# Fused two-block kernel on one core: the first stage, the ends of two loops and the mixer's loop in another order

## The chip, the cores and the metric

One core of a Trainium2 chip runs the whole kernel; the other cores are idle. The metric is the device time of one launch in microseconds (us). The engines are named as in the profile: PE is TensorE, DVE is VectorE, ACT is ScalarE, POOL is GpSimd, SP is SyncE, which only issues DMAs here.

## What is computed

Two blocks over 512 tokens of 1024 channels, all in float32. Cut to the parts at issue:

```python
# first block, layer 0 (16 heads of 128), layer 1 (Fourier, 8 groups of 256 channels)
sh, sc, gt = split(silu(cvec) @ ada_w + ada_b)            # modulation, from c and from c_ctx
h = rms_norm(x) * (1 + sc) + sh                           # for 512 tokens and for 256 context tokens
q, f1, f2, v, z = h @ w_in                                # per head
o = chunk_scan(forwards) + chunk_scan(backwards)          # gated linear recurrence
x = x + gt * ((rms_norm(o) * silu(z)) @ hg_w_out)         # E = 2048 -> D = 1024
u, z = split(h @ ft_w_in);  y = fft2(u).real * silu(z)
x = x + gt * (y @ ft_w_out)                               # E = 2048 -> D = 1024
# second block: x = x + swiglu/2; x = x + token_mixer(rms_norm(x)); x = x + swiglu/2; rms_norm
# token_mixer: six projections, 4-tap conv + RG-LRU scan, GLU + 31-tap conv + layernorm, two gates
```

## The kernel before, in words

Activations lie with channels on the 128 partitions and tokens along the free axis, so a product is made of 128x128 weight tiles against up to 512 tokens. To keep float32 accuracy each factor is split in two fp32r parts, the rounded upper half (`hi`) and the remainder (`lo`), and each tile takes three matmuls: hi x hi, hi x lo, lo x hi (`three`, L436).

**The weight stream.** All big weights come as a stream of blocks of eight tiles (512 KB, `BLK` = 1024 columns), in the order in which PE wants them. There are two slots. For each block SP loads `w_raw` when the slot's `lo` was made (L392); ACT copies it to `w_hi` (`cut`, L881) once the block two earlier in the same slot has been used (`after(k)` waits for block k and cuts block k+2); DVE subtracts to make `w_lo` (L1360); PE's `take` waits for that and its last matmul of the block frees the slot (`w_used`). Every engine works through its own list in the order that is written out in the code, and a waiting instruction holds up all behind it on its engine.

**First stage (L384 to L505, L922 to L946, L1418 to L1482).** SP loads the vectors, then x (2 MB), then four parts of the modulation weights (2 MB each). POOL loads the context (1 MB), masks, identity and the first gate weights. ACT squares x and the context, one 128x512 tile at a time through one buffer, `st_sq`, and DVE adds them up. PE computes the modulation with 64 matmuls (L498), the first mean (L480) in front of the fourth part and the second mean after all. DVE copies the four result rows out of PSUM, inverts the first root (L1462), copies the last row, makes the `lo` halves of blocks 0 and 1, adds biases, and then goes through both norms: for each tile one scalar_tensor_tensor (x times scale times inverse root, L1384), ACT makes `hi` with the shift (L901), DVE makes `lo` (L1387). The second root and its inverse stand between the two norms. PE's first real product waits for these tiles.

**Heads (a Fori of 15 and one ending).** `pe_head(i, j)` projects head i (five blocks, in parts a, b, c, and the modulation of layer 1) in between the steps of the scan of head j. The last call has no head i: there `begin_output(k, part)` puts the first half (tiles of heads 0 to 7) of the first four blocks of the output projection into parts a and b. After it come the other halves of those four (tiles of heads 8 to 15, each waits with `as_cut` until the last y is split), then four more channel tiles of two blocks each (`residual`). A channel tile that is done is added to x by DVE, squared by ACT, and the squares summed by DVE.

**Fourier mixer (a Fori of 7 groups and one ending).** `pe_group(i, j)` projects group i (four blocks, `project(0..3)`) between the transforms of group j: `turn`, `over_tokens(0, 1)`, `over_channels(0, 1)`. The last call has nothing to project. Its output projection (16 blocks) starts after all y are split (L736, `dve_ft`). Then POOL loads 64 KB of meta tokens and DVE and ACT make small sums from them before the residual starts.

**Mixer's loop (a Fori of 4, L797 on PE, L1230 on ACT, L1970 on DVE).** Each iteration uses 14 blocks: six against 528 tokens (two banks), six against 512, and two (`RG_A`, `RG_X`) of which only the first four of eight tiles hold anything. ACT does the activations, DVE a 4-tap convolution, the scan and its products, and 62 taps of the long convolution (`some_taps(n)`, one instruction each, L1963), placed by hand between the splits of blocks. PE's block k waits for `w_lo` of that block.

## Time and profile before

| what | us |
|---|---|
| median of 3 runs | 2650.39 |
| lowest and highest | 2647.41, 2652.21 |
| the profiled execution, its own time | 2652.72 |
| span in the profile | 2651.0 |
| PE busy | 2517.7 (95%) |
| DVE busy | 1629.7 (61%) |
| ACT busy | 1001.7 (38%) |

The profiled execution is one run: its own time is 1.7 us above its span. A matmul's end is modelled, so "busy" of PE counts short tails behind a last matmul; the distance from one start to the next is the surer measure. The granted clock (PEclk) is 1.00 at 2.4 GHz and 0.50 at 1.2 GHz; 0.98 is its mean over the run.

### The profile page before, as it was taken

How to read it: one execution, taken by the hardware profiler on the slowest of the kernel's cores; microseconds unless marked ns; L12 is line 12 of the kernel's file. 1: busy time of each engine (PE TensorE's matmuls, PEld its weight loads, DVE VectorE, ACT ScalarE, POOL GpSimd, SP SyncE). 2: the span in 40 equal slices, each digit the busy share in tenths (PEclk: the TensorE clock that was granted, in tenths of full speed). 3: DMA queues.
4: the chain of work that ended last, by engine and by line, in shares of the span. 5: the costliest groups of instructions: out<-in, count | busy, mean ns of one | idle time of the engine just before them, and what ended most of it. 6: DMA issues, size and time to landing. Idle time of an engine off the chain costs nothing.

```text
span 2651.0 us, 40390 instructions
## 1 busy us (share of the span) xinstructions
PE 2517.7 (95%) x14488; PEld 2172.3 (82%) x14488; DVE 1629.7 (61%) x2380; ACT 1001.7 (38%) x1350; POOL 113.7 (4%) x140
## 2 busy tenths in 40 slices
PE   6999999999999988999899999989999999999996
PEld 1788888888888875888689999989888878888885
DVE  5567777777777655444446343457999985544445
ACT  3334443444335323333235322235455543322222
POOL 0011211111111100000000000000000000000000
PEclk9999999999999998999899999989999999999998
DMA  5121222122212222222122222222222222222222
GB/s 227 64 72 57 77 71 71 56 79 71 71 55 79 95 80 65 78 72 78 49 95 86 88 90 92 87 95 88 87 84 90 90 84 95 88 95 95 95 95 87
DMA packets 59818, 223.83 MB, mean 84 GB/s; under 512 B 6496, under 2 KB 6496, under 8 KB 59264
## 3 DMA queue, kind: packets, MB, share of 16 engines
q1 hardware_dynamic: 56544, 207.94, 23.7%
q0 software_dynamic: 3232, 15.34, 1.6%
q8 instruction: 26, 0.43, 0.1%
q14 instruction: 16, 0.13, 0.0%
HBM read 221.15 MB, written 2.10 MB: 84 GB/s over the span
## 4 chain that ended last, share of the span: by engine, by line
PE 84%; DVE 7%; issue 4%; ACT 4%; DMA 1%; DVEq 0%; ACTq 0%; SPq 0%; POOL 0%
PE ps L441 73%; PE ps L600 4%; PE ps L622 1%; PE ps L498 1%; DVE w_lo L1360 1%; DVE cv L1963 1%; ACT L976 1%; DMA ada_raw<-in_ada_weights_dram 1%; PE ps L641 1%; PE ps L613 1%; PE ps L632 1%; PE ps L587 1%; PE ps L634 1%; PE ps L633 1%; DVE n_tmp L1963 0%
## 5 line engine op out<-in xcount | busy, mean ns | idle before, releaser
L881 ACT ACTIVATE w_hi<-w_raw 128x1024 fp32r<-128x1024 f32 x360 | 381.3, 1059 | 997.5 <-PE ps L441 991.9
L1360 DVE TENSOR_TENSOR w_lo<-w_raw,w_hi 128x1024 fp32r<-128x1024 f32 x360 | 439.3, 1220 | 223.8 <-ACT w_hi L881 221.7
L441 PE MATMUL ps<-n_hi,w_hi 128*128 128x512 f32 (+1 forms) x992 | 323.1, 357 | 27.9 <-DVE w_lo L1360 16.3
L441 PE MATMUL ps<-n_lo,w_hi 128*128 128x512 f32 (+1 forms) x992 | 320.3, 355 | 0.0
L441 PE MATMUL ps<-n_hi,w_lo 128*128 128x512 f32 (+1 forms) x992 | 319.9, 354 | 0.0
L441 PE MATMUL ps<-h_hi,w_hi 128*128 128x512 f32 x640 | 273.6, 427 | 8.3 <-DVE h_lo L1387 4.2
L441 PE MATMUL ps<-h_hi,w_lo 128*128 128x512 f32 x640 | 255.3, 399 | 0.0
L441 PE MATMUL ps<-h_lo,w_hi 128*128 128x512 f32 x640 | 254.9, 398 | 0.0
L441 PEld LDWEIGHTS ps<-n_hi,w_hi 128*128 128x128 f32 x992 | 175.1, 190 | 61.6 <-issue 20.5
L441 PEld LDWEIGHTS ps<-n_lo,w_hi 128*128 128x128 f32 x992 | 175.9, 190 | 27.1 <-issue 0.2
L441 PEld LDWEIGHTS ps<-n_hi,w_lo 128*128 128x128 f32 x992 | 175.9, 190 | 26.7
L441 PEld LDWEIGHTS ps<-h_hi,w_hi 128*128 128x128 f32 x640 | 121.8, 190 | 37.6 <-issue 9.6
L441 PEld LDWEIGHTS ps<-h_hi,w_lo 128*128 128x128 f32 x640 | 121.5, 190 | 29.2
L441 PE MATMUL ps<-xg_hi,w_hi 128*128 128x264 f32 x704 | 144.2, 286 | 0.0
L441 PE MATMUL ps<-xg_lo,w_hi 128*128 128x264 f32 x704 | 143.2, 285 | 0.0
L441 PEld LDWEIGHTS ps<-h_lo,w_hi 128*128 128x128 f32 x640 | 122.0, 191 | 25.1 <-issue 2.9
L441 PE MATMUL ps<-xg_hi,w_lo 128*128 128x264 f32 x704 | 142.3, 283 | 0.0
L441 PE MATMUL ps<-hid_hi,w_hi 128*128 128x264 f32 (+1 forms) x528 | 141.2, 321 | 0.0
L441 PE MATMUL ps<-hid_lo,w_hi 128*128 128x264 f32 (+1 forms) x528 | 141.0, 322 | 0.0
L441 PE MATMUL ps<-hid_hi,w_lo 128*128 128x264 f32 (+1 forms) x528 | 140.6, 320 | 0.0
L600 PE MATMUL ps<-Q,K_now 128*128 128x128 f32 x896 | 127.8, 286 | 5.3 <-ACT K_now L1008 3.6
L600 PEld LDWEIGHTS ps<-Q,K_now 128*128 128x128 f32 x896 | 118.4, 191 | 16.7 <-ACT K_now L1008 10.2
(342 smaller groups left out, 5052.7 us busy)
## 6 DMA issues: line engine op xcount, KB each, us to landing
w_raw<-in_weights_dram SPq DMA_DIRECT2D x376, 512.0 KB, 3.3
ada_raw<-in_ada_weights_dram SPq DMA_DIRECT2D x4, 2048.0 KB, 25.6
gate_raw<-in_gate_weights_dram POOLq DMA_DIRECT2D x16, 512.0 KB, 3.6
x<-in_x_dram SPq DMA_DIRECT2D x1, 2048.0 KB, 9.2
x<-in_x_dram POOLq DMA_DIRECT2D x1, 2048.0 KB, 8.0
out_dram<-fin POOLq DMA_DIRECT2D x1, 2048.0 KB, 6.5
xc<-in_ctx_dram POOLq DMA_DIRECT2D x1, 1024.0 KB, 10.6
masks<-in_masks_dram POOLq DMA_DIRECT2D x1, 512.0 KB, 12.8
```

What stands on the lines that cost most here:

```text
L441: last = nc.tensor.matmul(o, w, xp, start=start and n == 0, stop=stop and n == 2)
L498: last = nc.tensor.matmul(ps[0:2, n], csil[:, k], raw_[:, :, k * P:(k + 1) * P], start=k == 0, stop=k == KD - 1)
L587: last = nc.tensor.matmul(ps[:, 4, tile(t)], ksum[:, tile(t)], q_st[:, tile(t)], start=True, stop=True)
L600: last = nc.tensor.matmul(ps[:, 5 - l % 2, tile(t)], K_now[:, l % 2, tile(t)], woven(Q, t * P, P, 2 ** l, 1), start=True, stop=True)
L613: last = nc.tensor.transpose(ps[:, 6, tile(x)], K[:, d, tile(ORDER[d][n])], ident[:])
L622: last = nc.tensor.matmul(ps[:, 4 + g_ % 2, tile(x)], KT[:, x], V[:, ORDER[d][n]], start=True, stop=True)
L632: nc.tensor.matmul(o, V[:, CT + t], ST[:, t], start=True, stop=False)
L633: nc.tensor.matmul(o, states[:, 1 + t, 0], Q[:, 0, tile(t)], start=False, stop=False)
L634: last = nc.tensor.matmul(o, states[:, 4 - t, 1], Q[:, 1, tile(t)], start=False, stop=True)
L641: nc.tensor.matmul(ps[:, 5], ones_h[:], osq[:], start=True, stop=True).then_inc(pe_scan, 1)
L881: run(w_hi[:, s], w_raw[:, s], ACT.Copy).then_inc(hi_ready[s], 1)
L1360: tt(w_lo[:, s], w_raw[:, s], w_hi[:, s].bitcast(F32), ALU.subtract).then_inc(lo_ready[s], 1)
```

## The change

1. **First stage.** SP's queue becomes: vectors, modulation part 0, x, part 1, context, parts 2 and 3. POOL waits for the context before it loads the identity, and for part 3 before the masks. The squares go through two buffers. The mean of x stands inside part 1 of the modulation and the context's mean behind it. ACT instead of DVE copies the modulation rows. DVE multiplies x and the context by their inverse roots in place before the modulation is there (`over_root`), so that after it ACT makes `hi` straight from x with scale and shift, and DVE makes a tensor_scalar and a subtraction.
2. **Ending of the heads.** 16 half blocks instead of 8 go between the steps of the last scan: first the tiles of heads 0 to 7 of four blocks, then those of heads 8 to 13 of four more. The tiles of heads 14 and 15 (two of each block) are split into a buffer of their own, `kept`, and multiplied at the end. The tile order of SP's loads is written out (`OUT_ORDER`); it names the same blocks. ACT and DVE get `early_after(k)` at eight places.
3. **Ending of the Fourier mixer.** `begin_output(k)` puts tiles of channels 0 to 1023 of four output blocks between the transforms of the last group; their other halves come right after, and only tiles 14 and 15 wait for the last y. SP loads those blocks in the order of `OUT_ORDER`. The residual's loops there are unrolled.
4. **Mixer's loop.** The two half-empty blocks are split only in their first 512 columns. On DVE, splits move ahead of taps and between the two scans; on ACT, the split and activation of the last block move ahead of the last two copies.

```diff
-            sp.dma_start(x0[:], x_in).then_inc(x_in_s, 16)
             for n, (dst, a, b_) in enumerate(ADA_LOADS):
                 sp.dma_start(dst, ada_in[a:b_].rearrange("b p n -> p b n")).then_inc(ada_loaded[n], 16)
+                if n == 0:
+                    sp.dma_start(x0[:], x_in).then_inc(x_in_s, 16)
+                elif n == 1:
+                    sp.dma_start(xc[:], ctx_in).then_inc(xc_in_s, 16)
...
             for n, (raw_, a, b_) in enumerate(ADA_LOADS):
-                if n == 3:
-                    mean(N0, T, st_sum[:, 0])
                 pe.wait_ge(ada_loaded[n], 16)
                 for k in range(KD):
+                    if n == 1 and k == KD - 2:
+                        mean(N0, T, st_sum[:, 0])
                     last = nc.tensor.matmul(ps[0:2, n], csil[:, k], raw_[:, :, k * P:(k + 1) * P],
                                             start=k == 0, stop=k == KD - 1)
                 last.then_inc(ada_part, 1)
+                if n == 1:
+                    mean(N0C, TC, st_sum[:, 1], bank=5)
...
+            def over_root(N, x, rt_):
+                dve.wait_ge(N["root"], 1)
+                own.link(v.reciprocal(rt_, rt_))
+                for k in range(KD):
+                    tt(x[:, k], x[:, k], rt_, ALU.mult).then_inc(N["tmp"], 1)
+
+            over_root(N0, x0, st_sq[:])
             cut(0)
             cut(1)
+            over_root(N0C, xc, st_tmpc[:, 2])
...
+            def first_lo(N, x, n, tmp, hi, lo):
+                for k in range(KD + 1):
+                    if k < KD:
+                        if k > 1:
+                            dve.wait_ge(N["lo"], k - 1)
+                        own.mark(ts(tmp(k), x[:, k], scale[:, n, k:k + 1], ada0[:, k, n:n + 1], ALU.mult, ALU.add))
+                    if k:
+                        own.wait(1 if k < KD else 0)
+                        dve.wait_ge(N["hi"], k)
+                        tt(lo(k - 1), tmp(k - 1), hi(k - 1).bitcast(F32), ALU.subtract).then_inc(N["lo"], 1)
...
+                def begin_output():
+                    k, n = next(parts)
+                    xs = as_cut({"lo": y_cut}, whole(y_hi, y_lo))
+                    if n == 0:
                         s = take(k)
                         pe.wait_ge(acc_free, HEADS * 6 + 2)
+                    at, half = k // EARLY * KD, (KD - (LATE if k >= EARLY else 0)) // 2
+                    last = tiles(k % 2, [ps[:, k % EARLY]], xs, range(at + half * n, at + half * (n + 1)),
+                                 k < EARLY and n == 0, False, half * n)
+                    if n:
+                        last.then_inc(w_used[k % 2], 1)
...
+            pe.wait_ge(kept_s, EARLY)
+            for n in range(LATE):
+                t = HEADS - LATE + n
+                pe.wait_ge(y_cut, t + 1)
+                for k in range(EARLY):
+                    last = three([ps[:, k]], kept_hi[:, k, n * P:(n + 1) * P], kept_lo[:, k, n * P:(n + 1) * P],
+                                 [y_hi[:, t]], [y_lo[:, t]], False, n == LATE - 1)
+                    if n == LATE - 1:
+                        last.then_inc(early_done, 1)
...
-            st.enter(0, EARLY)
             for k in range(EARLY):
-                st.wait_done(dve, k)
+                dve.wait_ge(early_done, k + 1)
                 stt(x1[:, k], ps[:, k], gates[:, k, 0:1], x1[:, k], ALU.mult, ALU.add).then_inc(RC["res"], 1)
-                after(k)
                 add_square(RC, k, *sums)
...
-                project(0); turn(); project(1); over_tokens(0); over_tokens(1)
-                project(2); over_channels(0); project(3); over_channels(1)
+                project(0); turn(); project(1); begin_output(0); over_tokens(0); begin_output(1); over_tokens(1)
+                project(2); begin_output(2); over_channels(0); project(3); begin_output(3); over_channels(1)
...
-            pe.wait_ge(dve_ft, GROUPS * 8 + 1)
-            residual(RF, KD // 2, 2, whole(y_hi, y_lo), T)
+            for k in range(EARLY):
+                s = take(k)
+                tiles(s, [ps[:, k]], last_y, range(KD, 2 * KD), False, True).then_inc(w_used[s], 1)
+            residual(RF, (KD - EARLY) // 2, 2, whole(y_hi, y_lo), T, done=EARLY)
...
-                after(4)
+                after(4, BLK // 2)
                 for a in range(2):
                     actv(1 + a)
...
                     actv(3 + a)
                     tt(ii[:, a], ii[:, a], xr[:, a], ALU.mult)
                     stt(pp[:, a], (gvs, ggs)[a][:], 1.0, pp[:, a], ALU.add, ALU.mult).then_inc(mx_dve, 1)
-                some_taps(4)
                 after(11)
+                some_taps(3)
                 for a in range(2):
                     actv(5 + a)
                     own.link(tt(ii[:, a], ii[:, a], pp[:, a], ALU.mult))
                     own.link(v.tensor_tensor_scan(pp[:, a], rr[:, a], ii[:, a], 0.0, ALU.mult, ALU.add))
                     staged(7 + a)
                     tt(yst[:, a], yst[:, a], pp[:, a, META:TM], ALU.mult).then_inc(mx_dve, 1)
-                some_taps(2)
-                after(12)
-                some_taps(6)
+                    after(12 + a)
+                    some_taps((2, 1)[a])
                 for a in range(2):
                     actv(7 + a)
                     tt(row(a_lo, i * 2 + a), yst[:, a], row(a_hi, i * 2 + a).bitcast(F32), ALU.subtract
                        ).then_inc(mx_dve, 1)
-                after(13)
-                some_taps(7)
+                some_taps(4)
                 after(14)
-                some_taps(len(taps))
+                some_taps(6)
```

The numbers of taps between the other splits of an iteration are, in order, 5, 6, 4, 6, 4, 6, 3, 8 and 4 (before: 5, 5, 4, 6, 3, 6, 2 and 2, 2 and none); the two half splits are those of `RG_A` and `RG_X`.

## Rows read from the trace of the kernel before

**Rows 1.** The page, part 1: busy us (share of span), instructions

```profile
PE 2517.7 (95%) x14488; PEld 2172.3 (82%) x14488; DVE 1629.7 (61%) x2380; ACT 1001.7 (38%) x1350; POOL 113.7 (4%) x140
```

**Rows 2.** Busy time of each engine in stretches of the span (first line: columns)

```profile
core 0: us, PE busy (x) PEld busy (x) DVE busy (x) ACT busy (x) POOL busy (x), PEclk, DMA share, GB/s
...
20.00:36.00 16.00, 16.00 (x33) 2.93 (x32) 4.76 (x11) 3.96 (x9) 0.00 (x0) 1.00 1.02 409
...
102.20:902.90 800.70, 789.72 (x4833) 692.96 (x4832) 581.12 (x927) 342.63 (x508) 103.72 (x120) 1.00 0.21 68
902.90:981.90 79.00, 68.13 (x320) 55.75 (x319) 47.88 (x61) 23.19 (x33) 6.42 (x10) 0.91 0.31 104
...
1049.00:1270.40 221.40, 221.40 (x1142) 186.82 (x1142) 106.29 (x213) 79.29 (x134) 0.00 (x0) 1.00 0.22 74
1270.40:1293.80 23.40, 10.68 (x58) 9.72 (x56) 11.42 (x25) 6.11 (x13) 0.00 (x0) 0.71 0.07 23
...
1889.40:1970.50 81.10, 75.64 (x481) 68.02 (x481) 74.58 (x103) 43.63 (x52) 0.00 (x0) 1.00 0.28 91
...
2110.40:2168.00 57.60, 49.18 (x197) 37.63 (x196) 53.37 (x73) 22.11 (x29) 0.00 (x0) 0.97 0.25 83
```

**Rows 3.** Chain that ended last, first 103 us: start us, us, what

```profile
1.80 17.77 DMA ada_raw<-in_ada_weights_dram
...
43.77 6.97 PE ps L498 x16
...
54.13 0.76 DVE st_tmp L1384
...
77.91 24.26 PE ps L441 x120
```

**Rows 4.** Timeline of the first stage: start us, us, instruction, idle before

```profile
10.56 0.63 ACT L908 ACTIVATE st_sq<-x 128x512 f32<-128x512 f32 x1 [4.77 <-DMA x<-in_x_dram]
...
12.34 0.69 DVE L1371 TENSOR_TENSOR st_sum<-st_sum,st_sq 128x512 f32<-128x512 f32 x1 [0.69 <-ACT st_sq L908]
...
45.87 3.35 DVE L1462 RECIPROCAL st_sq<-st_sq 128x512 f32<-128x512 f32 x1 [2.44 <-ACT st_sq L895]
```

**Rows 5.** The same chain in the last head: start us, us, what

```profile
905.96 5.46 PE ps L441 x12
...
912.07 2.79 PE ps L441 x12
...
954.57 1.14 PE ps L641 x2
...
962.76 37.29 PE ps L441 x152
```

**Rows 6.** Timeline of the Fourier ending, and DVE's last sum on meta tokens

```profile
1274.77 1.94 PE L703 MATMUL ps<-ident,u_st 128*128 128x128 f32 x8 [4.22 <-DVE y_lo L1789]
...
1300.22 0.17 DVE L1858 TENSOR_SCALAR both_sum<-both_sum 128x16 f32<-128x16 f32 x1
```

**Rows 7.** The chain there: start us, us, what

```profile
1287.32 0.39 ACT o_sb L1141
...
1293.84 6.32 PE ps L441 x19
```

**Rows 8.** Waits within one iteration of the mixer's loop: us, times, longest

```profile
PE ps L441 <- DVE w_lo L1360: 5.8, 4, 2.2
...
DVE ii L2025 <- ACT gvs L1289: 2.8, 1, 2.8
```

**Rows 9.** Instructions by tile: count, ns min/median/max, first and last start, forms

```profile
L1959 DVE TENSOR_SCALAR cv<-vpad,vec x8: 545/546/548, 1807.2 to 2089.2; 128x512 f32 x8
...
L2040 DVE TENSOR_TENSOR a_lo<-yst,a_hi x8: 678/682/686, 1873.3 to 2117.0; 128x512 f32 x8
```

**Rows 10.** The page, part 5: groups, busy us and mean ns, idle before

```profile
L881 ACT ACTIVATE w_hi<-w_raw 128x1024 fp32r<-128x1024 f32 x360 | 381.3, 1059 | 997.5 <-PE ps L441 991.9
L1360 DVE TENSOR_TENSOR w_lo<-w_raw,w_hi 128x1024 fp32r<-128x1024 f32 x360 | 439.3, 1220 | 223.8 <-ACT w_hi L881 221.7
```

More of the change, by code:

```diff
@@ L53 @@
 Z_BANK = 2
+BLOCKS_TO_OUT = HEADS * 6 + 2 * KD + 4 * GROUPS
+OUT_ORDER = [BLOCKS_TO_OUT + 2 * m + n for n in range(2) for m in range(EARLY)]
+LATE = 2
 EPS = 1e-6
@@ L202, in program @@
         h_hi, h_lo = h.take("h_hi", [P, KD, T], F32R), h.take("h_lo", [P, KD, T], F32R)
+        kept = h.over()
+        kept_hi, kept_lo = [kept.take(f"kept_{n}", [P, EARLY, LATE * P], F32R) for n in ("hi", "lo")]
         hc_hi, hc_lo = h.take("hc_hi", [P, KD, TC], F32R), h.take("hc_lo", [P, KD, TC], F32R)
@@ L467, in bank2, with mean @@
                 return [ps[:, b, 0:HALF], ps[:, b + 1, 0:HALF]]
-            def mean(N, n, src, added=None):
+            def mean(N, n, src, added=None, bank=6):
                 if added:
@@ L479, in mean @@
                 else:
-                    last = nc.tensor.matmul(ps[:, 6, 0:n], ones_d[:], src[:, 0:n], start=True, stop=True)
+                    last = nc.tensor.matmul(ps[:, bank, 0:n], ones_d[:], src[:, 0:n], start=True, stop=True)
                 last.then_inc(N["mean"], 1)
@@ L506, in _ @@
             last.then_inc(ada_done, 1)
-            pe.wait_ge(N0["root"], 1)
-            mean(N0C, TC, st_sum[:, 1])
+            pe.wait_ge(N0C["root"], 1)
             def tile(t):
@@ L673, in residual @@
                 st.leave(trips)
-            st.enter(0, EARLY)
-            for k in range(EARLY):
-                s = take(k)
-                tiles(s, [ps[:, k]], as_cut({"lo": y_cut}, whole(y_hi, y_lo)), range(8, 16), False, True
-                      ).then_inc(w_used[s], 1)
-            st.leave(1)
             residual(RC, (KD - EARLY) // 2, 2, whole(y_hi, y_lo), T, done=EARLY)
@@ L880, in cut, with after @@
                 act.wait_ge(w_used[s], use + 1)
-                run(w_hi[:, s], w_raw[:, s], ACT.Copy).then_inc(hi_ready[s], 1)
-            def after(k):
+                run(w_hi[:, s, 0:n], w_raw[:, s, 0:n], ACT.Copy).then_inc(hi_ready[s], 1)
+            def after(k, n=BLK):
                 st.wait_done(act, k)
-                cut(k + 2)
+                cut(k + 2, n)
             def fetch_root():
@@ L1148, in act_group @@
                 hi(1, u_hi[:, 1], ps[:, 5])
+                if i is None:
+                    after(0)
                 stage(0)
@@ L1296, in _ @@
                 out_of(12, row(gate[:, 0], i * 2 + 1), ACT.Sigmoid, b_in(4, 1))
+                after(13)
+                out_of(13, row(gate[:, 1], i * 2 + 1), ACT.Sigmoid, b_in(5, 1))
                 for a in range(2):
@@ L1299, in _ @@
                     run(row(a_hi, i * 2 + a), yst[:, a], ACT.Copy).then_inc(mx_act, 1)
-                after(13)
-                out_of(13, row(gate[:, 1], i * 2 + 1), ACT.Sigmoid, b_in(5, 1))
             st.leave(KD // 2)
@@ L1797, in dve_group @@
                 next_block(1)
+                if i is None:
+                    after(0)
                 fold(1)
@@ L2041, in _ @@
                        ).then_inc(mx_dve, 1)
-                after(13)
-                some_taps(7)
+                some_taps(4)
                 after(14)
-                some_taps(len(taps))
+                some_taps(6)
+                assert not taps
             st.leave(KD // 2)
```

284 lines of the change are left out of this document (172 added, 112 removed).

## The prediction

> **What bounds the kernel.** The page's first line shows PE at work in 95% of the span, DVE in 61%, ACT in 38% [rows 1]. So the kernel is PE's work plus the stretches in which PE waits: 2651.0 less 2517.7 us is 133 us, the most that a change of order alone could bring. Next comes the view by stretches, read for where PE's busy time falls short of the stretch, or its clock below 1.00 [rows 2]. In the loop over heads and in seven Fourier groups PE has next to nothing to gain. Four places are left: the first 78 us, the last head (11 us idle and a mean clock of 0.91 in 79 us), the last Fourier group (10.7 us busy in 23.4, clock 0.71), and each iteration of the mixer's loop (75.64 busy in 81.1) with the stretch after it. The change works on these four. The chain, the timelines and the waits give the prices.
>
> A unit for all that follows: twelve 512-wide matmuls take 2.79 us at full clock, 0.233 each, so a block of 24 takes 5.58; at half clock twelve take 5.46 [rows 5].
>
> **First stage.** The chain begins with 17.8 us of waiting for modulation part 0 [rows 3], because x is loaded in front of it. The loads run at 409 GB/s while the queues are full [rows 2], and data flows from about 2.3 us on. In the new order, by bytes (0.3 MB of vectors, 2.1 per part, 2.1 for x, 1.05 of context): part 0 lands at 2.3 + 2.4/0.409 = 8.2 us, x at 13.3, part 1 at 18.4, context at 21, part 2 at 26.1, part 3 at 31.2. PE needs 6.97 us per part at full clock [rows 3]; part 0 is finished well before 18.4 even with its slow first matmuls. From there PE is the bound: 18.4 + 3 x 6.97 and the two means (1.06 and 0.7) is 41 us, against 43.77 + 6.97 = 50.7. The copy of the last row, 16 transposes, bias and scale took 3.4 us before (50.7 to 54.13, with a pair of weight splits beside them) and take 2.5 now, so modulation is ready at 43.5 instead of 54.1.
>
> DVE must have done its new work by then: squares of x end at about 20 us (13.3, then eight at 0.69 [rows 4]), of the context at 25; the root follows at 27; inverse 3.35 [rows 4]; eight products of x at 0.69, one row's price for a 512-wide tensor_tensor; two splits at 1.22; then the context's inverse (half as wide, 1.7) and eight products (0.4 each). That is 27 + 3.35 + 5.5 + 2.4 + 1.7 + 3.2 = 43.1: it just fits under PE, and each us that it is late is a us lost. Behind the modulation DVE needs per tile one tensor_scalar and one subtraction instead of two scalar_tensor_tensors of 0.75. The tensor_scalar is 0.546 alone in the trace and less when queued [rows 9]; its bounds are 0.4 and 0.75; I take 0.42 of DVE's time, so 1.04 per tile against 1.45. Eight tiles are 8.3 us and eight of the context 5.3, and the inverse of 1.7 between them is gone: DVE is through at 57.5. PE ends block 0 at 53.2 (bound to DVE), block 1 with 24 more matmuls at 58.8 and its context part (24 of half width, 2.8) at 61.6, when ACT and DVE have block 2 and its Silu ready. Before, this point was 77.91 [rows 3]. The idle time in front of it also cost a clock drop: 120 matmuls took 24.26 us, where 72 at 0.233 and 48 at half of that are 22.4. Gain: 16.3 + 1.9 = **18.2 us**; bounds 12 (DVE late, tensor_scalar at 0.75) and 20.
>
> Here a rule speaks against the row. The Trainium skill (DMA: Bandwidth & Descriptors, Specifications) puts a core's share of HBM at about 358 GB/s. By it part 3 would land at 35.3 us, 1.4 us after PE could begin it, and this gain would be 16.8. The row has 409 GB/s over 16 us, so the measurement is used.
>
> **Last head.** A head of the loop takes 800.7/15 = 53.4 us [rows 2]. Of that 120 wide matmuls are 27.9, 72 half-wide 8.4, modulation 0.9; the scan's own are 16.2. The last call starts at 905.96, as before: it waits for the gates [rows 5], and the clock falls there as before (2.7 us lost in the first twelve). Up to the norm (`L641`) it now holds eight half blocks of 12 and six of 9 matmuls: 22.3 + 12.6 + 16.2 + 2.7 = 53.8. One new wait: DVE's split of block 7 stands ahead of the last state (`passed(2)`), and waits for ACT, which waits for the eleventh half block; PE's output step comes about 0.9 us late. So the norm ends at 960.7; before, it ended at 954.57 + 1.14 = 955.7 [rows 5]. The last y takes 7.05 us from there (955.7 to 962.76), 8.0 now, since ACT and DVE have the split of block 8 in front (DVE's 1.22, half of it exposed): 968.7. PE has two half blocks and twelve kept matmuls meanwhile, 7.0 us, so it idles 1 us. Then twelve matmuls (2.8) finish all four tiles at once, and here is what is late next: the block after them waits for three of the four additions to x. Behind the last y DVE has a split (1.14), two clears (1.0), addition, sum, addition, sum, addition (five at 0.6 to 0.75): 5.6 us, of which PE covers 2.8. Next block at 974.3. Before: 75 matmuls from 962.76, 17.5 us and 1.7 for a half clock, 981.9. Gain **7.6 us**. The eight extra splits and four small ones (128x256, not in the trace: between 0.2 and 0.68) cost nothing while PE's half blocks hide them (DVE 47.9 us busy in 79); uncovered they would cost up to 1.9 + 1.5 us at each of four steps, so bounds 1 and 11.
>
> **Last Fourier group.** The 4.22 us in front of its transposes stay [rows 6], for the filler comes behind them. Then 0.9 of transposes, 48 transform matmuls (5.8 at half width), and four half outputs at 5.58: 29.0, plus 2.2 for a clock that has fallen, is 1306.0. Before, the last y came 5.2 us after the last transform (o_sb at 1287.32 to 1293.84, and the matmuls' tail) [rows 7]; now 0.3 more for a split. PE has 21 matmuls, 4.9 us, to hide it; the last tile starts at 1311.5. A new stop follows: PE's third of these blocks needs DVE's split, which stands behind the sums on meta tokens. They ended at 1300.39, 6.9 us after the last y [rows 6], were hidden by two blocks and now meet 6.3 us: with an addition and a split DVE is 9.0 us behind the y, a stop of 2.5. So 1311.5 + 0.7 + 3 x 5.58 + 2.5 + 8 x 5.58 = 1376.1, against 1293.84 + 16 x 5.58 + 1.8 (half clock) = 1384.9. Gain **8.8 us**, bounds 5 and 12.
>
> **Mixer's loop.** PE's work is about 74.6 us of an iteration: 75.64 less the tails of four stops. It stops for DVE's splits (5.8 us in four waits), and DVE stops 2.8 for ACT's squares [rows 8]. DVE is busy 74.58 of 81.1 [rows 2], so it is nearly as full as PE, and only orders badly: a run of taps or the two scans stand ahead of a split that PE wants. In the new order the splits come first and four taps fill the 2.8 us. The half splits save DVE 2 x (1.22 - 0.68) = 1.08 [rows 9, 10]; the price of a 512-wide split is bounded by 0.68, a like subtraction, and 1.22. DVE then needs 73.5 and hand-overs of about 1. I take 75.2 for an iteration: 5.9 x 4 = 23.6. After the loop, 197 matmuls hold 46.7 us of work in 57.6 [rows 2]; DVE enters that stretch earlier by its two taps and the moved scans, of which I take 1.5 (0 to 3). Gain **25.1 us**, bounds 16 and 28.
>
> The rest (unrolled loops, semaphores, gate weights behind the masks) I put at nothing: their cover is PE's queue, and the masks still land by 36 us. An unrolled loop may give or cost a few tenths.
>
> **Sum:** 18.2 + 7.6 + 8.8 + 25.1 = 59.7 us off the profiled execution's own 2652.72, 2593.0; the median of runs is 2.3 lower, so 2590.7.
>
> **Rivals.**
> - *DVE bounds the mixer's loop.* For it: 73.5 us of instructions with hand-overs against 74.6. If 3 us of waits stay in DVE's list, an iteration is 77.5, four give back 9: 2600. Against: its one long wait has taps in front now. Chance 0.14.
> - *The loads share instead of queueing.* If part 0 moves along with x and part 1 it lands near 25 us, PE ends the modulation at 57, and the first stage brings 2 instead of 18: 2607. Against: x was used at 10.56 [rows 4], part 0 nine us later. Chance 0.05. (The Trainium skill, DMA: Bandwidth & Descriptors, Queues, rings and completion order, says that descriptors of a ring are taken in order; by that rule this rival is out, and the trace agrees.)
> - *The fillers don't fill:* the endings stay bound by the chain through ACT and DVE, whose added splits take what PE gains. Both bring nothing: 2607. Against: PE's half blocks in the loop hide the same steps. Chance 0.06.
> - *Slower:* fuller work makes the chip grant the low clock within the mixer's loop. At a mean of 0.75 its 299 us of PE work would take 100 us more, 2690; it decides from 120 us at half clock on. Against: 221 us with PE without a pause ran at 1.00 [rows 2]. Chance 0.02.
>
> **Numbers.** The forecast has 0.73. Its own bounds make 2580 to 2605; with the first rival and the edge of the next the range is 2580 to 2609. 0.2% is 5.3 us, about what a measurement of this kernel can tell from no change. Every case but the last is faster by more: 0.97; within 0.01; slower 0.02.
>
> **What would show it.** Part 0's first matmul near 8 us and the third block of head 0 near 62; no tap group in PE's waits of the mixer's loop and a period of 75 to 76; short waits before the block behind the kept matmuls (3 us) and in the third block behind the last Fourier group (2.5 us), and none of 5 us left between. The sum is wrong if DVE's busy share of the loop nears 99% with PE still waiting, if the first product starts later than 48 us, or if PE's clock drops where it fell before in spite of the work.

## The result and the profile after

| what | us |
|---|---|
| median of 4 runs (lowest, highest) | 2609.29 (2604.83, 2612.46) |
| median of the kernel before beside them | 2650.49 |
| ratio, 95% interval | 0.9841, 0.983 to 0.9852 |
| predicted (range) | 2590.7 (2580 to 2609) |
| the profiled execution: its own time, span | 2606.13, 2604.4 |

The change brings 41.2 us by the medians. The forecast was 59.7, and the median lies 0.3 us above the upper end of its range. The two profiled executions stand 46.6 us apart: the one of before is 2.2 above the median beside it, the one of after 3.2 below. All that follows from traces is against these 46.6.

The four runs of the kernel after lie in two pairs, 2604.83 and 2606.13 at a mean granted clock of 0.985 and 0.986, 2612.45 and 2612.46 at 0.982. Their median falls between the pairs, so a difference of two medians can be some us off, and where a stage's time in two traces can be had, it is the surer measure. One later run of the kernel before took 3769.82 us at a granted clock of 0.617 and is in no median here.

The page of the kernel after, part 1 (beside [rows 1]):

```profile
PE 2505.3 (96%) x14488; PEld 2165.1 (83%) x14488; DVE 1625.9 (62%) x2396; ACT 1002.4 (38%) x1358; POOL 113.7 (4%) x139
```

PE does the same work with 12.4 us less "busy": I take those for half clock and for the tails behind stops, which no run separates. The larger part of the gain is in its waits. To see where, take the start of the first matmul of each stage in both traces and subtract:

| stage (from its first matmul to that of the next) | before | after | gained | predicted |
|---|---|---|---|---|
| launch to the first product of head 0 | 56.57 | 46.69 | 9.9 | |
| head 0 | 48.16 | 42.17 | 6.0 | 18.2 with the line above |
| 15 heads of the loop | 801.23 | 800.14 | 1.1 | 0 |
| last head, output, first norm | 134.34 | 124.22 | 10.1 | 7.6 |
| seven Fourier groups | 234.47 | 234.41 | 0.1 | 0 |
| last group, output, feed-forward | 511.61 | 500.11 | 11.5 | 8.8 |
| mixer's loop | 326.40 | 318.01 | 8.4 | 23.6 |
| behind the loop, to layer norm's products | 55.26 | 55.71 | -0.5 | 1.5 |
| from there to the last matmul | 463.55 | 463.60 | 0.0 | 0 |

Three of the four parts came within 3 us of their price. The mixer's loop brought a third of its own. Forecast and trace are 13.1 us apart (59.7 and 46.6); the loop and the stretch behind it lack 17.2, and the other stages together gave 4 more than forecast.

The view by stretches of the kernel after, whose rows answer to [rows 2]:

```profile
core 0: us, PE busy (x) PEld busy (x) DVE busy (x) ACT busy (x) POOL busy (x), PEclk, DMA share, GB/s
88.86:889.00 800.14, 788.63 (x4831) 691.51 (x4831) 581.08 (x928) 342.75 (x511) 104.29 (x120) 1.00 0.21 69
889.00:1013.20 124.20, 108.87 (x512) 87.81 (x513) 71.82 (x90) 36.47 (x50) 6.41 (x10) 0.95 0.29 98
1247.60:1747.70 500.10, 487.52 (x3618) 467.64 (x3618) 234.37 (x286) 163.06 (x188) 0.54 (x1) 0.99 0.27 88
1925.35:2003.80 78.45, 76.59 (x481) 69.56 (x481) 73.21 (x103) 41.70 (x50) 0.00 (x0) 0.98 0.29 94
2065.80:2121.50 55.70, 50.17 (x197) 38.83 (x197) 44.75 (x60) 20.79 (x27) 0.00 (x0) 0.94 0.23 76
```

The fourth row is one iteration of the mixer's loop: 78.45 us where 75.2 was forecast. PE has the 481 matmuls of [rows 2] and DVE its 103 instructions, and DVE's busy time fell from 74.58 to 73.21, a little more than priced (73.5). Neither engine is full, the clock is below 1.00, and there is a wait left. The waits of one iteration name it:

```profile
DVE w_lo L1454 <- issue: 3.0, 1, 3.0
PE ps L465 <- DVE w_lo L1454: 2.0, 1, 2.0
PE ps L465 <- ACT xpad L1338: 1.9, 1, 1.9
```

The two rows of PE are the stops at the stretch's two ends, one in each iteration. The first row is new: before one split DVE stands for 3.0 us with "issue" as the reason, which means that it waited for nothing that the profile shows. The timeline of DVE there:

```profile
1920.31 0.69 DVE L2098 TENSOR_TENSOR cv<-cv,n_tmp 128x512 f32 x1
1923.99 1.23 DVE L1454 TENSOR_TENSOR w_lo<-w_raw,w_hi 128x1024 fp32r<-128x1024 f32 x1 [2.99 <-issue]
```

The same two instructions in the kernel before:

```profile
1967.89 0.69 DVE L1967 TENSOR_TENSOR cv<-cv,n_tmp 128x512 f32 x1
1969.11 1.23 DVE L1360 TENSOR_TENSOR w_lo<-w_raw,w_hi 128x1024 fp32r<-128x1024 f32 x1 [0.53 <-DVE cv L1967]
```

Between the two stands DVE's jump back to the start of the loop. Seen in its own records, the jump is followed by the next instruction after 0.25 us in all three iterations of the kernel before, and after 2.80, 2.71 and 2.69 us in the kernel after. ACT had the other half of the split done at 1918.8, five us before DVE began, so this is no wait for ACT.

One more pair of rows differs: the page's part 3, the DMA queues that carry instructions. Before:

```profile
q8 instruction: 26, 0.43, 0.1%
q14 instruction: 16, 0.13, 0.0%
```

After:

```profile
q8 instruction: 28, 0.46, 0.1%
q14 instruction: 31, 0.25, 0.0%
```

Queue 14 brings 15 packets more, of 8 KB each. The DMA view narrowed to one iteration (1925.35 to 2003.80) has five of them:

```profile
q14 instruction: 5, 0.04, 0.2%
```

That of the kernel before (1889.4 to 1970.5) has no such row. The five start at 1928.0, 1959.4, 1998.0, 2000.5 and 2002.9, and the jump is at 1999.57. Between the second and the third DVE ran some 130 instructions. No view names queue 14 as DVE's; I read it from this timing.

This gave **theory F**: DVE holds only so many blocks of 128 instructions. The mixer's loop has 270 of them before and 268 after. Counted over all of DVE's instructions, waits and registers too, it stands at 781 to 1050 before and at 838 to 1105 after, because the change unrolls loops and adds splits ahead of it. If blocks begin at about 843, 971 and 1099, as the packets say, the old place touches three and the new one four; one block more is brought ahead, and what is dropped for it is the one that the jump needs. (How many blocks are held and which one is dropped is a picture; no view shows it.) The rival, **theory W**: DVE's first split is late for a reason of order (PE's block, ACT's list), and the place is nothing to it.

### The profile page after: what moved, and what is told of

Same layout as the page of the kernel before. It is cut to its first block, busy times and chain, and to the rows that moved or that the text cites. A ratio compares the mean times of both kernels' runs of the same rounds, so it can differ in the third digit from the quotient of the medians.

```text
span 2604.4 us, 40290 instructions
## 1 busy us (share of the span) xinstructions
PE 2505.3 (96%) x14488; PEld 2165.1 (83%) x14488; DVE 1625.9 (62%) x2396; ACT 1002.4 (38%) x1358; POOL 113.7 (4%) x139
## 4 chain that ended last, share of the span: by engine, by line
PE 86%; DVE 5%; ACT 4%; issue 3%; DMA 1%; DVEq 0%; ACTq 0%; SPq 0%; POOL 0%
PE ps L465 76%; PE ps L630 4%; PE ps L652 1%; PE ps L522 1%; DVE w_lo L1454 1%; ACT L1060 1%; PE ps L643 1%; DMA ada_raw<-in_ada_weights_dram 1%; PE ps L671 1%; ACT w_hi L937 1%; PE ps L662 1%; PE ps L617 1%; PE ps L664 1%; PE ps L663 1%; DVE n_tmp L1478 0%
## 5 line engine op out<-in xcount | busy, mean ns | idle before, releaser
L937 ACT ACTIVATE w_hi<-w_raw 128x1024 fp32r<-128x1024 f32 (+1 forms) x360 | 378.1, 1050 | 1002.6 <-PE ps L465 992.1
L1454 DVE TENSOR_TENSOR w_lo<-w_raw,w_hi 128x1024 fp32r<-128x1024 f32 (+1 forms) x360 | 434.9, 1208 | 247.6 <-ACT w_hi L937 237.8
L630 PEld LDWEIGHTS ps<-Q,K_now 128*128 128x128 f32 x896 | 118.5, 191 | 14.8 <-ACT K_now L1092 10.2
```

Of the source, the lines that this page charges most:

```text
L630: last = nc.tensor.matmul(ps[:, 5 - l % 2, tile(t)], K_now[:, l % 2, tile(t)], woven(Q, t * P, P, 2 ** l, 1), start=True, stop=True)
L937: run(w_hi[:, s, 0:n], w_raw[:, s, 0:n], ACT.Copy).then_inc(hi_ready[s], 1)
L1454: tt(w_lo[:, s, 0:n], w_raw[:, s, 0:n], w_hi[:, s, 0:n].bitcast(F32), ALU.subtract).then_inc(lo_ready[s], 1)
```

## The experiments

Each was timed beside the kernel before on the same chip: medians of it were 2650.81 (the first four), 2650.47 (the next four) and 2651.54 (the last four).

**1. The kernel after, 40 instructions further back.**

```diff
+        shift = g.take("shift", [P, 40])
...
+            for n in range(40):
+                v.memset(shift[:, n:n + 1], 0.0)
             sum_squares(R0, KD, st_sum[:, 0], lambda k: st_tmp[:, k % 2])
```

> The kernel after, with 40 memsets of 128x1 on DVE between its set-up and the first sum of squares, where DVE stands idle for 5 us (10.2 to 15.3). They do nothing but move the mixer's loop 40 instructions further back in DVE's program. Theory F (instruction fetch): in the kernel after, the queue of instructions brings four or five packets of 8 KB in every iteration of the mixer's loop, two or three of them at DVE's jump back, and DVE stands 2.7 us behind the jump; in the kernel before it brings none there, and the jump costs 0.25. The loop has 268 instructions; the packets come when DVE's instructions number about 842, 970 and 1098 are reached, 128 apart, so the body (838 to 1105) lies in four such blocks, and 40 later (878 to 1145) it lies in three, as the body before did. Then: jump 0.25 to 0.3 us, no instruction packets in the second to fourth iteration, period 75.2 to 75.8 instead of 78.5, stop in front of the third block under 0.6 us, no half clock behind it, total 2597 to 2601 (after: 2609.3). Theory W (the 2.7 us are a wait: DVE's first split stands behind something that PE's block or ACT releases, and the place in the program is nothing to it): jump and period as in the kernel after, total 2608 to 2610.

Measured: 2595.89 (ratio to before 0.9793, 0.978 to 0.9807), 13.4 us less than the kernel after, by forty instructions that do nothing. The jump took 0.25, 0.23 and 0.23 us; no packet of instructions came in the second to fourth iteration. One iteration:

```profile
1843.90:1918.90 75.00, 74.97 (x483) 68.10 (x482) 73.18 (x102) 41.86 (x50) 0.00 (x0) 1.00 0.29 98
```

PE has no gap left in it, and the clock is 1.00. Theory F expected this; W expected no change. The total is a little below what F gave (2597 to 2601): the memsets' tile had also moved other tiles in SBUF (experiments 5 and 9).

**2. The kernel before, 56 instructions further back**, the same edit with 56. It puts the old loop where the new one stands.

> The kernel before, with 56 such memsets at the same place. Its mixer's loop (270 instructions) moves from 781 to 1050 to 837 to 1106, where the kernel after has its own, over four blocks. Theory F: the jump back rises from 0.25 to about 2.7 us, with instruction packets in every iteration; the split behind the jump is the one that PE waits for there (a stop of 1.88 us already), so PE's stop grows by about 2.5 us in each of three iterations, with a half clock behind it of up to 1.7 us: period 83.5 to 85, total 2658 to 2663 (before: 2650.5). Theory W: nothing changes in the loop, total 2649 to 2652.

Measured: 2661.82 (ratio 1.004, 1.0026 to 1.0054). The jumps took 2.84, 3.03 and 2.89 us. Part 3 of the page, and one iteration with its waits:

```profile
q14 instruction: 31, 0.25, 0.0%
```

```profile
1889.80:1974.90 85.10, 76.92 (x480) 69.51 (x480) 74.59 (x103) 42.30 (x50) 0.00 (x0) 0.98 0.26 87
```

```profile
PE ps L442 <- DVE w_lo L1361: 8.0, 3, 4.2
DVE w_lo L1361 <- issue: 3.3, 1, 3.3
```

The period rose from 81.0 to 85.1, by the fetch and by half a clock behind the longer stop. Nothing in this kernel's order was changed. Its tile of memsets moved all later tiles by 224 bytes, though, and that is not nothing either: the loop over heads took 796.95 us instead of 801.23, because the 256-wide matmuls that follow each other there without a stop started 117.5 ns apart on the mean instead of 122.2, and the last Fourier group with the feed-forward took 2.2 us more. So the total (11.0 us by medians) is not the price of the place alone. The mixer's loop as a stage is: 12.2 us more than before, and the same in kernel 4, where no tile moved.

**3 and 4. Each order of the mixer's loop in the other kernel.** Kernel 3 is the one of before with part 4 of the change alone; its loop stands at 781 to 1048. Kernel 4 is the one of after with the old loop, at 838 to 1107.

```diff
 before, kernel 3                                   after, kernel 4
-                after(4)                           -                after(4, BLK // 2)
+                after(4, BLK // 2)                 +                after(4)
...
-                some_taps(2)                       -                    after(12 + a)
-                after(12)                          -                    some_taps((2, 1)[a])
-                some_taps(6)                       +                some_taps(2)
+                    after(12 + a)                  +                after(12)
+                    some_taps((2, 1)[a])           +                some_taps(6)
```

> The kernel before with the new mixer's loop alone (half splits, taps redistributed, splits between the scans, ACT's order at the end). Its body lies at 781 to 1048, in three blocks, without any shift. Theory F: the part of the change is as I had priced it but for the end of the loop: period 75.2 to 75.8 against 81.0, three of them, and a stop of 4.2 us behind the last iteration as in the kernel after; gain 15 to 20 us, total 2631 to 2636. Theory W: the same as in the kernel after, where the part brought 8.5 us: period 78.4, total 2641 to 2643.

> The kernel after with the mixer's loop of the kernel before; the body lies at 838 to 1107, in four blocks. Theory F: old order and a jump of 2.7 us: period 83.5 to 85, total 2609.3 plus 8.5 plus 8 to 11, so 2626 to 2629. Theory W: period 81.0, total 2617 to 2619.

Measured: kernel 3 2634.52 (ratio 0.994, 0.9926 to 0.9953), jumps 0.25 to 0.27, an iteration of 74.9; kernel 4 2631.82 (0.9926, 0.9913 to 0.994), jumps 2.71 to 2.94. One iteration of each (kernel 3, then kernel 4):

```profile
1880.10:1955.00 74.90, 74.84 (x482) 67.89 (x482) 73.11 (x102) 41.85 (x50) 0.00 (x0) 1.00 0.29 98
```

```profile
1859.00:1945.00 86.00, 79.34 (x481) 72.01 (x482) 74.56 (x103) 42.34 (x50) 0.00 (x0) 0.95 0.25 86
```

With 1 and 2 this is a square. The mixer's loop as a stage, by starts of matmuls:

| | body over three blocks | body over four |
|---|---|---|
| old order | 326.40 (before) | 338.58 (2), 338.49 (4) |
| new order | 307.94 (3) | 318.01 (after) |

(Kernel 2 has its tiles moved; kernel 4, without that, has the same.) The new order is worth 18.5 us at one place and 20.5 at the other; the place is worth 10 to 12 in either order. Part 4 brought 8.4 because the two came together. Kernel 4's total is 3 us above what I expected: I had added a period's loss to the 8.5 us that part 4 had brought, and the difference between the orders is 20.5 there.

**5 and 6. Eight and 125 instead of 40.** They test the blocks by number.

> The kernel after with 8 memsets instead of 40: the mixer's loop lies at 846 to 1113, its first instruction just behind 843, where the packets say that a block begins. If whole blocks of 128 instructions decide (theory F), this is three blocks and as fast as 40 more: jump 0.25, period 74.9, total 2595 to 2598. If it is something that 40 memsets do in another way (the time that they take, a later sum of squares), 8 of them bring a fifth of the 13 us: 2604 to 2607.

> The kernel after with 125 memsets: the loop lies at 963 to 1230, over the blocks from 843, 971, 1099 and 1227, so over four again, with the last four instructions in the fourth. Theory F: the jump costs 2.7 to 2.9 again, instruction packets in every iteration, period 78.3 to 78.6, total 2606 to 2610. If more instructions in front are simply better, it stays at 2595 to 2597.

Measured: 8 more 2586.14 (0.9756, 0.9741 to 0.9771), jumps 0.25, and 16 packets in queue 14; 125 more 2607.94 (0.9842, 0.9827 to 0.9857), jumps 2.69 to 3.01. The page of 125 more:

```profile
q14 instruction: 32, 0.26, 0.0%
```

So it is not "more in front is better": 0 slow, 8 and 40 quick, 125 slow again, as the blocks of 128 have it. One thing these runs can't tell apart. A body of 268 lies over four blocks only where it starts in the last 11 places of one, which is worked out from the numbers above (843, 971, 1099), so "four blocks" and "starts just ahead of a block" name the same cases. The packets in the middle of the body (the one at 1959.4, far from any jump) speak for the first; a loop of another length would settle it. It also says that the change met this by bad luck, at 11 places of 128.

But 8 more was 10 us *better* than 40 more, which neither theory has. It gained in the stages that are full of wide matmuls: 3.8 us against 40 more in the loop over heads, 3.7 in the seven Fourier groups. The starts of 512-wide matmuls that follow each other without a stop (200 to 260 ns apart) stood 229.6 ns apart on the mean in the loop over heads, against 233.0 or 233.1 in before, after and 125 more, and 232.4 in 40 more. The memsets had a tile of their own, which had moved all later tiles in SBUF. Experiments 9 and 10 take the two apart.

**7. PE starts early behind the loop.** PE's timeline in the kernel after has this row behind the loop's last iteration:

```profile
2065.75 0.50 PE L465 MATMUL ps<-a_hi,w_hi 128*128 128x512 f32 x1 [3.82 <-DVE yst L2165]
```

It waits there for both products with the scans (4.2 us from start to start, where the kernel before has 2.6), though six of the eight rows that the block multiplies were ready.

```diff
-            pe.wait_ge(mx_dve, KD // 2 * 12 - 2)
             rnn_out((0, 1, 2, 3))
```

> The kernel of 40 more, and PE does not wait, before the block behind the mixer's loop, for both products with the scans. The block takes rows 0 to 5 first, which are ready; for rows 6 and 7 it waits where it needs them, as the code does already. Theory: the stop of 4.26 us in front of the block is covered by 18 matmuls (4.2 us), then a stop of 2 to 2.8 for row 6, which stands behind a split and a tap on DVE; the second block starts 1.5 to 2.2 us earlier. Rival: the next stops (2.33 and 1.21, for DVE's sums) grow by the same, because DVE is the one that is late, and the total stays at 2595 to 2597; otherwise 2593.5 to 2594.5.

Measured: 2593.24 (0.9785, 0.9772 to 0.9798), 2.65 below 40 more. PE's remaining stops there, by its timeline:

```profile
2060.55 0.50 PE L466 MATMUL ps<-a_hi,w_hi 128*128 128x512 f32 x1 [0.27 <-DVE yst L2167]
2062.95 0.50 PE L466 MATMUL ps<-a_hi,w_hi 128*128 128x512 f32 x1 [1.44 <-DVE a_lo L2172]
```

From the loop's last matmul to the products behind the layer norm it takes 56.6 us against 60.8, more than the 1.5 to 2.2 that I had given it, since row 6 was only 1.44 late. The next stop (2.28 from start to start, against 2.33) did not grow, so the rival falls: DVE was late for this one point alone. Of the 4.2 us the medians show 2.65, with intervals that overlap, so the gain is shown by the stage and not by the total. The two profiled executions are equal (2597.12 and 2597.08), since the last head took 4.0 us more in this one: the clock fell once more there, at 956.8, which the edit does not reach.

**8. Whole splits instead of half ones.**

```diff
-                after(4, BLK // 2)
+                after(4)
...
-                after(7, BLK // 2)
+                after(7)
```

> The kernel of 40 more with whole splits in place of the two half ones, which costs DVE 1.06 us more (1.22 against 0.69) and ACT 0.86 in each iteration. With 40 more PE is busy 74.97 of 75.0 us and DVE 73.2, with 0.3 at the jump and about 0.8 in front of its first tap: 0.7 us are left. Theory: DVE runs out of room, a stop of 0.3 to 0.5 us comes in each iteration and the stop behind the loop grows by about 1: total 2597 to 2599. Rival: the half splits bring nothing, since PE sets the pace, 2595 to 2596.5.

Measured: 2602.45 (0.9818, 0.9805 to 0.9832), 6.6 us more than 40 more, beyond what either side expected. One iteration, and PE's waits over the loop:

```profile
1846.70:1922.65 75.95, 75.03 (x481) 67.98 (x481) 74.23 (x103) 42.66 (x50) 0.00 (x0) 1.00 0.30 97
```

```profile
PE ps L466 <- DVE w_lo L1455: 2.8, 5, 0.7
```

The period rose by 0.95, DVE's busy time by 1.05: nearly all of what DVE does beyond its 73.2 us reaches the period. So with half splits DVE has next to nothing to spare beside a full PE. The profiled executions are 5.4 us apart: 3.5 in the mixer's loop, and 2.9 in the last head, where the clock fell once more (at 954.3, for 3.4 us); the edit doesn't reach that stage, and I leave that part open.

**9 and 10. The place alone, and addresses alone.**

```diff
 kernel 9                                           kernel 10
+            for n in range(40):                    +        shift = g.take("shift", [P, 8])
+                v.memset(st_tmpc[:, 2, n:n + 1], 0.0)
```

> The 40 memsets again, now into a column range of a tile that exists already (the scratch tile of the context's root), so that no tile moves in SBUF. With 40 more and 8 more the memsets had a tile of their own, which moved every tile behind it by 160 and 32 bytes, and in those two runs the 512-wide matmuls of the loop over heads came every 232.0 and 229.4 ns on the mean, against 233.0 in the kernels before, after and 125 more. Theory: two things were mixed, DVE's place in the program and SBUF addresses. The place alone gives jump 0.25, period 75.0 to 75.2, no packets, and matmuls 233.0 ns apart: total 2597.5 to 2600. Rival: the matmuls' pace has another cause (the memsets, the chip), and the total is that of 40 more, 2595 to 2597.

> The kernel after with an unused tile of 32 bytes behind the tile of zeros, and no memset: every later tile lies 32 bytes further in SBUF, nothing in any engine's program moves. Theory (addresses): matmuls of the heads' loop 229.4 ns apart and of the Fourier groups 227.8, jump still 2.7 us and period about 78.4; total 2609.3 less 9 to 11: 2598 to 2601. Rival (the pace of 8 more came from something else): pace 233.0, total 2605 to 2611.

Measured: place alone 2597.1 (0.9796, 0.9782 to 0.981); addresses alone 2593.77 (0.9787, 0.9773 to 0.9801), more than the 9 to 11 us that I had given it. One iteration of the first, and its page's part 3:

```profile
1844.30:1919.20 74.90, 74.86 (x483) 67.96 (x482) 73.15 (x103) 41.79 (x50) 0.00 (x0) 1.00 0.30 98
```

```profile
q14 instruction: 17, 0.14, 0.0%
```

The loop over heads and the seven Fourier groups, in kernel 9 and then in kernel 10:

```profile
89.30:889.30 800.00, 788.53 (x4830) 691.32 (x4831) 581.04 (x928) 342.51 (x511) 104.27 (x120) 1.00 0.21 70
1013.40:1247.80 234.40, 229.33 (x1160) 191.25 (x1161) 117.98 (x230) 85.11 (x143) 0.00 (x0) 0.99 0.22 72
```

```profile
88.60:885.30 796.70, 785.06 (x4830) 693.79 (x4830) 582.57 (x928) 342.53 (x511) 103.52 (x120) 1.00 0.21 70
1006.60:1237.00 230.40, 224.48 (x1161) 190.60 (x1161) 117.98 (x230) 85.13 (x143) 0.00 (x0) 0.99 0.22 73
```

The same matmuls at the same clock, and 3.3 and 4.0 us less. By lines, the products with the weights in the Fourier groups:

```profile
L465 PE MATMUL ps<-g_lo,w_hi 128*128 128x512 f32 x256 | 102.1, 399 | 0.0
```

```profile
L466 PE MATMUL ps<-g_lo,w_hi 128*128 128x512 f32 x256 | 100.4, 392 | 0.0
```

Each is 7 ns shorter in kernel 10. Its jumps took 2.71 us and its queue 14 brought 31 packets, as in the kernel after. So the two effects are separate: 12.2 us for the place (9.7 between the profiled executions, 10.2 in the mixer's loop as a stage), 15.5 for 32 bytes (15.0). Of the 15.0, 9.5 are in stages full of wide matmuls (3.4 heads, 4.0 Fourier groups, 2.1 behind the layer norm), as expected; the last head, the mixer's loop and the stretch behind it add 3.0, 1.1 and 2.5, and the last Fourier group with the feed-forward takes 1.0 back. Those are no clean effect of the addresses: in this execution the clock did not fall at the start of the last head or at the stops of the mixer's loop (1.00 for an iteration, against 0.98 in the kernel after).

**11. All three together**: kernel 9's memsets, the tile of 32 bytes, the early start.

> The kernel after with DVE's loop 40 instructions further back, the 32 bytes, and PE's early start behind the loop. Sum of what was measured apart: 2586.1 (8 more) less 2.6 to 4.2: 2582 to 2583.5. If the addresses are not the cause of the better pace, 2592 to 2597.

Measured: 2583.69 (0.9742, 0.9728 to 0.9755). It is 25.6 us below the kernel after and has the lowest median of all, 2.5 under 8 more, though the two intervals overlap. It leaves nothing of the computation out.

**12. x loaded first again**, on kernel 9.

```diff
+            sp.dma_start(x0[:], x_in).then_inc(x_in_s, 16)
             for n, (dst, a, b_) in enumerate(ADA_LOADS):
                 sp.dma_start(dst, ada_in[a:b_].rearrange("b p n -> p b n")).then_inc(ada_loaded[n], 16)
-                if n == 0:
-                    sp.dma_start(x0[:], x_in).then_inc(x_in_s, 16)
-                elif n == 1:
+                if n == 1:
                     sp.dma_start(xc[:], ctx_in).then_inc(xc_in_s, 16)
```

> The kernel of 40 instructions further back without moved tiles, and x loaded ahead of modulation part 0 again; all else of the new first stage stays (context behind part 1, constants late, sums and roots under the parts). Part 0 then lands 5 us later, at 13.4 by 4.5 MB at 405 GB/s from 2.35. PE has 6.97 us for a part, 2.9 more for the first seven matmuls at half clock: part 0 ends at 23.3, and the others and the two means (22.8) at 46.1 against 42.2. Theory (PE is the bound behind part 0): 3.5 to 4 us slower than the kernel with place alone. Rival 1 (the later parts' landing is the bound, and part 0's early start is idle time moved): no difference. Rival 2: the whole 5.2 us.

Measured: 2600.98 (0.9813, 0.9799 to 0.9827), 3.9 above place alone. PE's first products:

```profile
14.97 14.24 PE L521 MATMUL ps<-ada_raw,csil 128*2 128x512 f32 x28 [14.97 <-DMA ada_raw<-in_ada_weights_dram]
...
50.83 0.77 PE L464 MATMUL ps<-h_hi,w_hi 128*128 128x512 f32 x1 [2.41 <-DVE h_lo L1587]
```

The first product of head 0 starts 3.7 us later (50.83 against 47.11): the theory's 3.5 to 4. Only that much of the first stage's 15.9 comes from loading part 0 ahead of x. The other 12 belong to the rest of the new stage (context and constants later in the queue, the norms' work under the products), which no run took apart.

## Why the prediction was right or wrong

The direction and three of four parts were right. The mixer's loop was not: 7.9 us lie far below its own bounds (16 to 28), while the other three lie within theirs. That the total still came to the edge of the range is luck. The range reached 2609 for two rivals that did not come as described, and stages with nothing to do with the loop gave 4.1 us more than forecast. The range was also narrower than its parts: the four lower bounds together are 34 us, or 2616, and not 2605.

The loop failed at one sentence, "The rest (unrolled loops, semaphores, gate weights behind the masks) I put at nothing: their cover is PE's queue", with "a few tenths" for an unrolled loop. The unrolled loops and the added splits ahead of it moved DVE's longest loop by 57 instructions, and that cost 10 to 12 us in another stage (experiments 2, 3, 4 and 9). No cover hides it: DVE was nearly as full as PE there.

**Mixer's loop, 25.1 predicted, 7.9 measured.** PE's work of 74.6 us was right: 74.9 without a stop. "I take 75.2 for an iteration" holds where the body lies over three blocks. Two smaller parts were off too. I multiplied a steady iteration's 5.9 by four; the old loop's first iteration had one stop less, and behind the last one a stop of 4.2 us took the place of one of 2.6: the splits and taps that now stand between the scans make the second product late, which I read from DVE's list and no run tried. Kernel 3's stage gains 18.5 instead of 23.6. And the stretch behind the loop lost 0.5 instead of gaining 1.5; with the early start of experiment 7 the two together gain 21.1. The first rival, DVE as the bound, was there in part: 3 us of waits stayed in DVE's list, as it said, though they are a fetch and no hand-over; it gave 77.5 for an iteration, 78.45 was measured. The half splits, priced at 1.08 us of DVE's time, were worth 0.95 in the period (experiment 8).

The rule that speaks against this part stands in the Trainium skill (Runtime: NRT & Kernel Launch, Instruction fetch mechanics): instructions come in blocks, the next one is fetched ahead, and a taken branch whose target is outside the two pages held waits for a fetch. The traces agree in kind, with 2.7 to 3.0 us for the jump. They differ in the size: the page has blocks of 256 instructions (16 KiB), and the packets on DVE's queue here are of 8 KB, one for each 128 or so.

**First stage, 18.2 predicted, 15.9 measured.** PE's timeline and the view by stretches:

```profile
9.84 9.76 PE L522 MATMUL ps<-ada_raw,csil 128*2 128x512 f32 x16 [9.84 <-DMA ada_raw<-in_ada_weights_dram]
19.76 5.31 PE L522 MATMUL ps<-ada_raw,csil 128*2 128x512 f32 x12 [0.15 <-DMA ada_raw<-in_ada_weights_dram]
...
46.69 0.77 PE L465 MATMUL ps<-h_hi,w_hi 128*128 128x512 f32 x1 [2.41 <-DVE h_lo L1586]
```

```profile
2.35:9.80 7.45, 0.00 (x0) 0.00 (x0) 4.46 (x30) 1.93 (x5) 0.00 (x0) 1.00 1.02 383
9.80:19.80 10.00, 9.80 (x17) 1.60 (x18) 3.87 (x9) 4.28 (x7) 0.00 (x0) 1.00 1.00 414
```

The loads queue, as said (part 0 at 9.84, so the second rival is out), at 383 GB/s at first and 414 later. Part 0 came 1.6 us after my 8.2 and part 1 at 19.76 after my 18.4, and these 1.4 us go through to the end of the products (42.4 against 41). The rest is DVE's pair of instructions per tile, which I had priced at 1.04:

```profile
46.58 0.55 DVE L1582 TENSOR_SCALAR st_tmp<-x,scale,ada 128x512 f32<-128x512 f32 x1
47.04 0.68 DVE L1586 TENSOR_TENSOR h_lo<-st_tmp,h_hi 128x512 fp32r<-128x512 f32 x1
47.76 0.55 DVE L1582 TENSOR_SCALAR st_tmp<-x,scale,ada 128x512 f32<-128x512 f32 x1
```

It is 1.18, so 1.1 us more over eight tiles. The rate of the Trainium skill that I had weighed (358 GB/s) is not what the rows show. Its sum was also done wrongly: at that rate part 1 would land 2.3 us later, PE is the bound from there, and the gain would be 15.9 and not 16.8. That it is the measured number is chance, since the loads ran at 383 and 414 GB/s and 1.1 us of the loss is DVE's.

**Last head, 7.6 predicted, 10.1 measured.** The three stops came where they were put. PE's timeline:

```profile
935.94 0.49 PE L662 MATMUL ps<-ST,V 128*128 128x128 f32 x2 [0.69 <-DVE states L1705]
...
949.65 0.50 PE L465 MATMUL ps<-y_hi,kept_hi 128*128 128x512 f32 x1 [0.88 <-DVE y_lo L1727]
...
955.11 0.50 PE L465 MATMUL ps<-y_hi,w_hi 128*128 128x512 f32 x1 [2.43 <-DVE x L1834]
```

Forecast were 0.9, 1 and 2.8. The term that was mis-sized is the stretch in front: from the first half block to the sums of the norm it took 51.8 us (889.00 to 940.83), priced at 54.7. One us of that is the clock, which cost the first twelve matmuls 1.8 us instead of 2.7:

```profile
889.00 4.58 PE ps L465 x12
894.01 2.80 PE ps L465 x12
```

How much of the 2.5 us is the change is open, for the clock differs between executions. Of the kernels with the same code and addresses in this stage, number 9 took 124.1 us, but numbers 4 and 12 took 127.0 and 127.2, with the clock at half for 6.8 us at its start instead of 3.4 and for 3.4 more at its middle. Against those the stage gained 7.1 to 7.3.

**Last Fourier group, 8.8 predicted, 11.5 measured.** The 4.22 us in front of the transposes stayed to the hundredth. The stop in the third block behind was 1.1 us where I had 2.5, and the clock was at half for 3.4 us only (1.7 lost, 2.2 priced). These two are 1.9 of the 2.7.

**Fillers that don't fill, and a low clock in the loop**, the other two rivals, did not come: the endings gained more than forecast, and the mixer's loop without stops ran at 1.00.

## What to carry to other kernels

On DVE here, a loop of 268 instructions had a second cost beside its work: where it stands. For a loop of more than two blocks of 128 instructions, count all of the engine's instructions up to it in the built program, and look at the packets of the instruction queue per iteration. If there are any, shift the loop by a few instructions that fall into idle time (40 brought 10 to 12 us here, and with 8 an iteration took the same 74.9) before judging any change of its order. Let them write into a tile that exists: a tile of their own moves all later ones, which here was worth up to 15 us by itself. Other engines and other lengths were not tried. And never price an edit elsewhere on the engine at nothing without this look: unrolling a loop ahead moves every loop behind it.

## What the hardware showed that I had not expected

- A jump back of a loop of 268 to 270 instructions costs DVE 0.25 us where the body touches three blocks of 128 instructions, and 2.7 to 3.0 where it touches four: 0 and 125 instructions more in front are slow, 8 and 40 quick.
- Moving all later tiles by 32 bytes in SBUF brought the starts of 512-wide matmuls 3.2 ns closer together in the heads (233.0 to 229.8) and 5.4 in the Fourier groups (233.1 to 227.7), at the same granted clock, and made the kernel 15.5 us faster. Moved by 160 bytes it was 0.6 ns in the heads, by 512 nothing. Moved by 224 bytes (kernel 2) the 512-wide ones did not gain and the 256-wide ones of the heads came 4.7 ns closer. Which pair of tiles it is, and why, was not tried.
